# The last block's down product from seven block products instead of eight

## The chip, the cores and the metric

The kernel runs on one core of a Trainium2 chip. A core has TensorE (PE, matrix products into the PSUM memory), VectorE (DVE), ScalarE (ACT), GpSimd (POOL), the queue engine SyncE (SP), and 16 DMA engines that all queues share. The metric is device time in microseconds (us) of one execution; three runs are taken and the median counts.

## What is computed

One layer of a trunk on x of 2048 rows by 1024 columns, in float32: RMSNorm, a combined projection, two attention mixers, gates, an output projection with a residual, and then the part that the change touches:

```python
h2 = _rmsnorm(x, norm2_g[layer])
ff = jax.nn.silu(jnp.einsum('bsd,df->bsf', h2, w_ffn_gate[layer])) * jnp.einsum('bsd,df->bsf', h2, w_ffn_up[layer])
x = x + jnp.einsum('bsf,fd->bsd', ff, w_ffn_down[layer])
return _rmsnorm(x, norm_f_g)
```

The hidden width D_FF is 2816, which is 22 tiles of 128; DEPTH and BATCH are 1.

## The kernel before

The rows are taken in four blocks of 512 (`ROWS`), and the program is written engine by engine, with waits on semaphores; `n(sem, key)` is the count at which the step named by the key is done. A float32 operand is split into a high part and a low part (`hi`, `lo`), and each product is made by three matmuls: high by high, high by low, low by high.

**Weights.** A planned list `JOBS` holds all weight tiles in their order of use, 512 KB each. SP loads job i into one of two buffers `WRAW` as soon as POOL has split job i-2 (L807). POOL (`split`, L984 and L986) waits for the load and for PE's end of job i-2, and then makes, in two halves, `WHI` (a copy, 128x512) and `WLO` (raw minus high, 128x512). PE waits for each half (`w_split`).

**Feed-forward of a block.** The 22 tiles go in three parts of 8, 8 and 6 (`PARTS`). For each tile i of a part, PE makes the gate job ("fg") and the up job ("fu"), 24 matmuls of 128x512 each, into a ring of four PSUM banks ("pair"). ACT takes Silu of the gate bank (L1973), DVE multiplies it with the up bank in place (L2525), ACT copies the product into `FFhi` (L1977), and DVE writes the remainder into `FFlo` (L2528). A gate bank is free again after the Silu, an up bank after `FFlo`.
After the tiles of a part come its down jobs ("fd"): `rows` multiplies the part's `FFhi`, `FFlo` (stationary) with the split weights, two tiles of 512 columns per job, for each half of the 1024 columns and for four row tiles. DVE adds the four finished banks of each half to `X1` (L2470). In a part of 8 these are 8 jobs, in the part of 6 they are 6.

**End.** In the last block ACT squares the rows after the last addition (L1919) and takes the root (L1926), DVE inverts it (L2481); POOL multiplies `X1` with the last norm's weights (L1008) and scales it (L1013) for a half of the columns, DVE does the other half (L2562), and SP stores the rows (L857).

In blocks 0 to 2 DVE and ACT also work on the next block's attention during the feed-forward. In block 3 they do not, and the regions of SBUF that attention uses are free then.

Of the kernel before, what the change touches and what calls it, by code (L numbers as in the profile page):

```python
# [26 lines left out]
P = 128  # L27
# [30 lines left out]
def trunk_program(nc, io, known):  # L58
# [18 lines left out]
    with ExitStack() as ctx:  # L77
# [129 lines left out]
        MGhi, MGlo = at("MGhi", [P, KT, ROWS], f32r, r3), at("MGlo", [P, KT, ROWS], f32r, r3 + 16384)  # L207
        FFhi, FFlo = at("FFhi", [P, SLOTS, ROWS], f32r, r3), at("FFlo", [P, SLOTS, ROWS], f32r, r3 + 16384)
# [5 lines left out]
        def sem(name):  # L214
            return ctx.enter_context(nc.semaphore(name))

        ident_in, const_in, ones_set = sem("ident_in"), sem("const_in"), sem("ones_set")
        ftab_ready, ftab_out, tab_in, taba_ready = (sem(s) for s in ("ftab_ready", "ftab_out", "tab_in", "taba_ready"))
        wu_hi, wu_ready = sem("wu_hi"), sem("wu_ready")
        const_first, eps_set, act_squared, dve_squared, act_scaled = (  # L220
            sem(s) for s in ("const_first", "eps_set", "act_squared", "dve_squared", "act_scaled"))
# [7 lines left out]
        h_ready, h_hi, h_split, h_used = sem("h_ready"), sem("h_hi"), sem("h_split"), sem("h_used")  # L229
        q_hi, q_ready = sem("q_hi"), sem("q_ready")  # L230
        k_hi, k_ready, kw_ready, iw_ready = sem("k_hi"), sem("k_ready"), sem("kw_ready"), sem("iw_ready")
        lat_ready, lat_norm, lat_hi, lat_split = sem("lat_ready"), sem("lat_norm"), sem("lat_hi"), sem("lat_split")
        v_hi, v_ready, vat_ready, carried = sem("v_hi"), sem("v_ready"), sem("vat_ready"), sem("carried")
# [7 lines left out]
        found_ready, tile_signed, big_set, root_loaded = sem("found_ready"), sem("tile_signed"), sem("big_set"), sem("root_loaded")  # L241
# [10 lines left out]
        o_step, o_ready, ot_ready = sem("o_step"), sem("o_ready"), sem("ot_ready")  # L252
# [11 lines left out]
        near_scored, near_masked, near_negmax, near_probs = (sem(s) for s in ("near_scored", "near_masked", "near_negmax", "near_probs"))  # L264
        near_turned, near_hi, near_ready, near_valued = (sem(s) for s in ("near_turned", "near_hi", "near_ready", "near_valued"))
        near_copied, near_summed, near_inverted = sem("near_copied"), sem("near_summed"), sem("near_inverted")
        near_normed, near_kept = sem("near_normed"), sem("near_kept")
        tabb_in, vb_in, comb_ready = sem("tabb_in"), sem("vb_in"), sem("comb_ready")
        out_done = [sem(f"out_done{j}") for j in range(JT)]
# [32 lines left out]

        def ffn_jobs(b, part):
# [4 lines left out]
            return jobs + row_jobs(("fd", part[0]), b, io["w_ffn_down"][0], part)  # L308
# [265 lines left out]
        def _(sp):  # L574
# [219 lines left out]
            for i, (key, src) in enumerate(JOBS):  # L794
# [8 lines left out]
                if width > P:  # L803
                    raw = WRAW[i % 2][:, :, :].rearrange("p (k s) c -> p k (s c)", k=k)
                else:
                    raw = WRAW[i % 2][:, 0:k, 0:width]
# [1200 lines left out]
        def _(dve):  # L2007
# [405 lines left out]
            for b in range(NB):  # L2413
# [101 lines left out]
                for p in range(KT // 2):  # L2515
                    lower_half(1, p)
# [110 lines left out]
```

## Time and profile before

| | |
|---|---|
| median of 3 runs | 3198.29 us (3196.85 to 3199.2) |
| span of the profiled execution | 3196.7 us, 1.6 us under the median |
| granted clock of TensorE | 0.999 of full speed |
| busy share | PE 99%, POOL 64%, DVE 57%, ACT 44% |
| feed-forward of block 3 | from about 2830 us to the end |
| last addition of DVE starts | 3188.35 us |

The span runs from the first to the last instruction; the median of the runs is device time and holds a little more. A busy share is taken over the whole span, so that the stage that is changed has to be read on its own. PE is the only engine that is busy all the time, and matmuls are pipelined: their time is read from the distance of their starts, not from the length of one.

### The profile page before, as it was taken

To read this page: it belongs to the slowest core of one execution; us is meant where nothing else is said; L and a number is where in the kernel's file an instruction comes from. 1 tells how busy PE (TensorE), PEld (TensorE's weight loads), DVE (VectorE), ACT (ScalarE), POOL (GpSimd) and SP (SyncE) were. 2 spreads that over 40 slices of the span, in tenths; PEclk is the share of its full clock that TensorE was granted. 3 is DMA by queue.
4 is the path that set the end of the run, shared out by engine and by line. 5 is a ranking of instruction groups with operands and counts; after the bars stand their busy time and mean duration, and the time that the engine had idled before them with its cause. 6 is when DMAs were issued, how large, how long until landed. Compare 5 with 4: busy or idle time off the path is not lost.

```text
span 3196.7 us, 44024 instructions
## 1 busy us (share of the span) xinstructions
PE 3156.0 (99%) x15678; PEld 2655.0 (83%) x15678; DVE 1814.8 (57%) x3706; ACT 1420.8 (44%) x2589; POOL 2036.0 (64%) x2201
## 2 busy tenths in 40 slices
PE   9999999999999999999999999999999999999998
PEld 7888888878878888888888888988888799888887
DVE  3335546537565545557666666967868689521111
ACT  3324435435473534337354534837655378320001
POOL 5666766665556666764666676366767922666676
PEclk9999999999999999999999999999999999999999
DMA  5765455355615333331533334163333500533332
GB/s 152 198 167 172 119 154 157 103 157 163 209 35 182 102 112 107 108 125 57 201 104 116 103 102 138 28 238 103 98 109 112 171 23 17 180 91 99 95 103 99
DMA packets 464201, 392.59 MB, mean 123 GB/s; under 512 B 29264, under 2 KB 394064, under 8 KB 463344
## 3 DMA queue, kind: packets, MB, share of 16 engines
q1 hardware_dynamic: 442544, 345.56, 36.0%
q10 hardware_dynamic: 21440, 44.22, 3.7%
q8 instruction: 126, 2.06, 0.3%
q14 instruction: 91, 0.75, 0.1%
HBM read 323.76 MB, written 62.81 MB: 121 GB/s over the span
## 4 chain that ended last, share of the span: by engine, by line
PE 92%; POOL 2%; ACT 2%; DVE 2%; issue 1%; DMA 1%; SPq 0%; POOLq 0%; ACTq 0%; DVEq 0%
PE BANK L1049 22%; PE BANK L1051 21%; PE BANK L1050 21%; PE LP L1049 4%; PE LP L1051 4%; PE LP L1050 4%; PE BANK L1330 3%; PE BANK L1355 2%; PE LP L1166 2%; PE LP L1165 2%; PE LP L1310 2%; PE LP L1311 2%; PE BANK L1357 2%; POOL WLO L986 1%; POOL WHI L984 1%
## 5 line engine op out<-in xcount | busy, mean ns | idle before, releaser
L986 POOL TENSOR_TENSOR WLO<-WRAW,WHI 128x512 fp32r<-128x512 f32 x912 | 1213.3, 1330 | 76.0
L984 POOL TENSOR_SCALAR WHI<-WRAW 128x512 fp32r<-128x512 f32 x912 | 639.6, 701 | 776.1 <-PE BANK L1051 622.1
L1049 PE MATMUL BANK<-H2hi,WHI 128*128 128x512 f32 x1376 | 538.7, 392 | 1.1 <-POOL WLO L986 1.1
L1050 PE MATMUL BANK<-H2lo,WHI 128*128 128x512 f32 x1376 | 535.9, 389 | 0.0
L1051 PE MATMUL BANK<-H2hi,WLO 128*128 128x512 f32 x1376 | 535.8, 389 | 0.0
L1049 PE MATMUL BANK<-HThi,WHI 128*128 128x512 f32 (+1 forms) x1024 | 405.1, 396 | 0.8 <-DVE QS L2044 0.5
L1050 PE MATMUL BANK<-HTlo,WHI 128*128 128x512 f32 (+1 forms) x1024 | 399.4, 390 | 0.0
L1051 PE MATMUL BANK<-HThi,WLO 128*128 128x512 f32 (+1 forms) x1024 | 399.3, 390 | 0.0
L1751 ACT ACTIVATE MASK<-SCD,THR 128x896 bf16<-128x896 f32 (+5 forms) x186 | 281.9, 1516 | 191.8 <-DVE THR L2104 164.6
L1051 PEld LDWEIGHTS BANK<-H2hi,WLO 128*128 128x128 f32 x1376 | 258.3, 188 | 54.4
L1049 PEld LDWEIGHTS BANK<-H2hi,WHI 128*128 128x128 f32 x1376 | 258.6, 188 | 53.3 <-issue 1.3
L1050 PEld LDWEIGHTS BANK<-H2lo,WHI 128*128 128x128 f32 x1376 | 258.6, 188 | 51.1
L2071 DVE TENSOR_SCALAR_CACHE_REDUCE MASK<-SCD,THR 128x640 bf16<-128x640 f32 (+2 forms) x192 | 278.1, 1486 | 3.4
L1739 ACT ACTIVATE RB<-LP 128x1024 f32<-128x1024 f32 (+7 forms) x176 | 143.4, 819 | 231.9 <-PE LP L1166 207.9
L2525 DVE TENSOR_TENSOR BANK<-BANK,SL 128x512 f32<-128x512 f32 x88 | 61.2, 696 | 325.7 <-PE BANK L1051 305.9
L2308 DVE SCALAR_TENSOR_TENSOR SCP<-RB,IW,SCP 128x1024 f32<-128x1024 f32 (+7 forms) x140 | 175.2, 1266 | 106.2 <-ACT RB L1739 105.2
L1051 PEld LDWEIGHTS BANK<-HThi,WLO 128*128 128x128 f32 (+1 forms) x1024 | 190.9, 186 | 42.8
L2237 DVE TENSOR_TENSOR PTlo<-BANK,PThi 128x512 fp32r<-128x512 f32 (+1 forms) x296 | 193.2, 659 | 57.5 <-ACT PThi L1680 56.4
L1049 PEld LDWEIGHTS BANK<-HThi,WHI 128*128 128x128 f32 (+1 forms) x1024 | 191.1, 187 | 38.8 <-issue 0.6
L1050 PEld LDWEIGHTS BANK<-HTlo,WHI 128*128 128x128 f32 (+1 forms) x1024 | 191.3, 187 | 36.9
L1633 ACT ACTIVATE LGb<-LGb,NMB 128x1024 f32<-128x1024 f32 (+7 forms) x192 | 174.1, 907 | 57.9 <-POOL NMB L905 54.8
L905 POOL TENSOR_SCALAR NMB<-MXB 128x1 f32<-128x1 f32 x112 | 32.6, 291 | 250.6 <-DVE MXB L2194 247.6
(314 smaller groups left out, 6457.6 us busy)
## 6 DMA issues: line engine op xcount, KB each, us to landing
WRAW<-in_w_in SPq DMA_DIRECT2D x124, 512.0 KB, 4.2
WRAW<-in_w_ffn_gate SPq DMA_DIRECT2D x88, 512.0 KB, 3.8
WRAW<-in_w_ffn_up SPq DMA_DIRECT2D x88, 512.0 KB, 3.8
WRAW<-in_w_ffn_down SPq DMA_DIRECT2D x88, 512.0 KB, 3.5
qsp<-QS SPq DMA_DIRECT2D x32, 512.0 KB, 5.8
WRAW<-in_w_out SPq DMA_DIRECT2D x32, 512.0 KB, 4.6
gates<-GS ACTq DMA_DIRECT2D x62, 256.0 KB, 2.2
GL<-gates ACTq DMA_DIRECT2D x48, 256.0 KB, 4.5
```

The costliest lines, as they stand in the source:

```text
L984: nc.gpsimd.tensor_scalar(hi, raw, 1.0, 1.0, ALU.mult, ALU.mult).then_inc(w_hi, 1)
L986: nc.gpsimd.tensor_tensor(lo, raw, hi.bitcast(f32), ALU.subtract).then_inc(w_split, 1)
L1049: nc.tensor.matmul(dst, whi, mhi, start=first, stop=False)
L1050: nc.tensor.matmul(dst, whi, mlo, start=False, stop=False)
L1051: return nc.tensor.matmul(dst, wlo, mhi, start=False, stop=last)
L1330: last = nc.tensor.transpose(dst[:, 2 * e + h, :], probabilities(b, kind, p, h, t), IDENT[:, :])
L1633: nc.scalar.activation(lg, lg, ACT.Exp, bias=NMB[:, slot, 0:1], accum_out=(ES if s else RS)[:, j, h0:h0 + 1]).then_inc(probs, made(probs, ...
L1739: nc.scalar.activation(RB[:, g % 2, 0:w], logits(("idx",) + key)[:, 0:w], ACT.Relu).then_inc(relu_ready, made(relu_ready, key))
L1751: nc.scalar.activation(mask_of(b)[:, j, 0:w], found_at(b, j)[:, 0:w], ACT.Sign, bias=THR[:, j:j + 1].bitcast(f32), accum_out=CNT[:, j:j + ...
L2071: last = stepped(nc.vector.tensor_scalar(junk[:, j, 0:w], found_at(b, j)[:, 0:w], threshold(j), None, op, ALU.add, accum_out=CNT[:, j:j + 1]))
L2237: nc.vector.tensor_tensor(PTLO[b][r][:, 0:w, :], trans(key)[:, 0:w, :], PTHI[b][r][:, 0:w, :].bitcast(f32), ALU.subtract).then_inc(pt_read ...
L2308: ins = nc.vector.scalar_tensor_tensor(s, r, iw, s, ALU.mult, ALU.add)
```

## The change

In the last block only (`SEVEN`), each part's down product is taken as a product of 2 x 2 blocks and made from seven block products in Strassen and Winograd's way. The left operand's blocks are even and odd tiles of the part by the upper and lower 256 rows; the right operand's are even and odd weight tiles by the two halves of the columns.

- Four of the seven right operands are differences of weight blocks. ACT loads the weights of a part once more, in units of 128x256 from four places, by two DMAs of 256 KB for each unit into one pair of buffers `RQ` (`load_unit`). DVE forms four differences of each unit (`sum_unit`) into `TRAW`; ACT copies them to `THI`, DVE writes the remainders `TLO` over `TRAW` (`lower_t`). There are 8 units in a part of 8 and 6 in the part of 6, two for each pair of tiles. A unit is loaded when the differences of the unit before are done.
- Three of the seven left operands are sums of blocks of the up result. DVE forms them in SBUF (`seven_low`): the product of Silu and up goes to `EVEN` or `ODD` instead of back into its bank, then one 128x256 difference for an even tile and three 128x256 sums for an odd one; ACT copies (`SThi`), DVE takes the remainder (128x768).
- An up bank is free again after that product (`ff_ready`) and no longer after the remainder.
- The other three right operands are plain weight blocks, which SP loads and POOL splits as before: 6 jobs for each part instead of 8 (or 6).
- PE (`seven_products`) makes the first two products in turns, pairs 0 and 1 of both and then the rest of both; each step is 6 matmuls. Two products share two banks and three stay in the bank on top of one another; DVE adds each product to `X1` (`add_products`), and PE waits for the addition two products before.
- At the end the two halves of the columns change places; the last product is made row tile by row tile.
- Some semaphores are merged into others of the same engine.

```diff
+        LEFT = ("a11", 0, 1, 2, "s3", "a12", "a22")
+        RIGHT = ((0, 0), 0, 1, (1, 1), 2, (1, 0), 3)
+        PLACE = (0, 1, 0, 1, 0, 1, 0)
+        OPENS = (True, True, False, False, False, True, False)
+        INTO = ((0, 0), (1, 1), (0, 1), (0, 1), (1, 1), (0, 0), (1, 0))
...
+            if seven(b, part):
+                return jobs + [(seven_key(b, part, m, a), every_other(w, part, *RIGHT[m], a))
+                               for m in range(7) if type(RIGHT[m]) is tuple for a in range(2)]
...
+            def seven_products(b, part):
...
+                steps = [(m, p, range(2)) for ps in (range(2), range(2, count)) for m in range(2) for p in ps]
+                steps += [(m, p, range(2)) for m in range(2, 6) for p in range(count)]
+                steps += ([(6, p, (jj,)) for jj in range(2) for p in range(count)] if part is PARTS[-1]
+                          else [(6, p, range(2)) for p in range(count)])
+                for m, p, jjs in steps:
...
+                    if m > 1 and p == 0 and jjs[0] == 0:
+                        pe.wait_ge(rows_added, n(rows_added, added_key(b, part, m - 2, 1)))
...
+                        pe.wait_ge(t_low, n(t_low, (b, part[0], p, right // 2)))
+                        mhi, mlo = THI[:, p, right, :], TLO[:, p, right, :]
+                    if type(left) is int:
+                        pe.wait_ge(s_low, n(s_low, (b, part[2 * p])))
...
-                        job(H2hi, H2lo, (ff_split, (b, i)), beside=beside_up, ring="pair")
+                        job(H2hi, H2lo, (ff_ready if seven(b, part) else ff_split, (b, i)), beside=beside_up, ring="pair")
...
+                def load_unit(part, u):
...
+                    if u or part[0]:
+                        act.wait_ge(t_summed, n(t_summed, (b, *((part[0], u - 1) if u else (part[0] - SLOTS, SLOTS - 1)), 3)))
...
+                    for h in range(2):
...
+                        act.dma_start(RQ[h][:, :, :], src).then_inc(t_in, 16)
+
+                def seven_high(part, i):
...
+                    if f % 2 == 0:
+                        act.wait_ge(s_made, n(s_made, (b, i)))
+                        nc.scalar.copy(FFhi[:, f, :]...
+                    else:
+                        act.wait_ge(ff_ready, n(ff_ready, (b, i)))
+                        nc.scalar.copy(FFhi[:, f, :], ODD[:, :, :].rearrange("p h r -> p (h r)")).then_inc(ff_hi, made(ff_hi, (b, i)))
+                        act.wait_ge(s_made, n(s_made, (b, i, 2)))
+                        nc.scalar.copy(SThi[:, p, :, :], STR[p // 2][:, p % 2, :, :]).then_inc(s_hi, made(s_hi, (b, part[2 * p])))
+                    if f:
+                        load_unit(part, 2 * f)
+                    p = pair_at(part, f - 1)
+                    if p is not None:
...
+                        for t in range(2):
+                            nc.scalar.copy(THI[:, p, 2 * t:2 * t + 2, :], TRAW[:, p, 2 * t:2 * t + 2, :]
...
+                            if i > part[0]:
+                                load_unit(part, 2 * (i - part[0]) - 1)
+                            seven_high(part, i)
...
+                def sum_unit(part, u):
...
+                    dve.wait_ge(t_in, n(t_in, (b, part[0], u)))
+                    for t, x, y in ((0, RQ[0][:, 1, :], RQ[0][:, 0, :]), (2, RQ[1][:, 1, :], RQ[0][:, 1, :]),
+                                    (1, RQ[1][:, 1, :], TRAW[:, p, 0, c]), (3, RQ[1][:, 0, :], TRAW[:, p, 1, c])):
...
+                        nc.vector.tensor_tensor(TRAW[:, p, t, c], x, y, ALU.subtract
...
+                def seven_low(part, i):
...
+                    if 0 < 2 * f - 1 < len(part):
+                        sum_unit(part, 2 * f - 1)
+                    full(("fu", b, i))
+                    dve.wait_ge(silu_ready, n(silu_ready, (b, i)))
...
+                        nc.vector.tensor_tensor(odd, bk[:, :], gate, ALU.mult).then_inc(ff_ready, made(ff_ready, (b, i)))
+                        dve.wait_ge(ff_ready, n(ff_ready, (b, i)))
+                        for k, x, y, op in ((0, EVEN[:, 2, :], ODD[:, 1, :], ALU.add), (1, raw[:, 0, :], EVEN[:, 0, :], ALU.subtract),
+                                            (2, ODD[:, 0, :], raw[:, 1, :], ALU.subtract)):
...
+                        nc.vector.tensor_tensor(FFlo[:, f, :], odd, FFhi[:, f, :].bitcast(f32), ALU.subtract
...
+                        nc.vector.tensor_tensor(low, raw, SThi[:, p, :, :].bitcast(f32), ALU.subtract
...
+                    if 2 * f < len(part):
+                        sum_unit(part, 2 * f)
+                    if pair_at(part, f + 1 - len(part) // 2) is not None:
+                        lower_t(part, f + 1 - len(part) // 2)
...
+                def add_products(part, before):
...
+                        for jj in range(2):
+                            dve.wait_ge(bank_full, n(bank_full, closed_key(b, part, m, jj)))
...
+                            nc.vector.tensor_tensor(c, bank(("sd", b, part[0], PLACE[m], jj))[:, :], c, ALU.add
```

## Rows read from the trace of the kernel before

**Rows 1.** the page: busy us, share of the span, instructions of each engine

```profile
PE 3156.0 (99%) x15678; PEld 2655.0 (83%) x15678; DVE 1814.8 (57%) x3706; ACT 1420.8 (44%) x2589; POOL 2036.0 (64%) x2201
```

**Rows 2.** stretches of block 3: PE, PEld, DVE, ACT, POOL busy (x), clock, DMA, GB/s

```profile
2900.00:3000.00 100.00, 100.00 (x442) 82.79 (x442) 12.49 (x18) 6.53 (x11) 69.82 (x74) 1.00 0.32 100
...
3100.00:3196.00 96.00, 88.31 (x390) 72.81 (x388) 17.04 (x28) 15.71 (x34) 67.00 (x68) 0.98 0.32 104
```

**Rows 3.** waits of that stage: who waited for whom, us, times, longest

```profile
DVE BANK L2525 <- PE BANK L1051: 188.2, 21, 10.2
...
POOL WHI L984 <- PE BANK L1051: 74.8, 50, 1.5
```

**Rows 4.** timeline, PE: start us, length us, instruction; two matmuls 24 apart

```profile
3180.67 0.39 PE L1049 MATMUL BANK<-WHI,FFhi 128*128 128x512 f32 x1
...
3186.11 0.39 PE L1049 MATMUL BANK<-WHI,FFhi 128*128 128x512 f32 x1
```

**Rows 5.** timeline, POOL: the split of a job (three of four), the next job's start

```profile
3144.96 0.62 POOL L984 TENSOR_SCALAR WHI<-WRAW 128x512 fp32r<-128x512 f32 x1 [1.50 <-PE BANK L1051]
3145.66 1.29 POOL L986 TENSOR_TENSOR WLO<-WRAW,WHI 128x512 fp32r<-128x512 f32 x1
3146.92 0.62 POOL L984 TENSOR_SCALAR WHI<-WRAW 128x512 fp32r<-128x512 f32 x1
...
3150.40 0.62 POOL L984 TENSOR_SCALAR WHI<-WRAW 128x512 fp32r<-128x512 f32 x1 [1.48 <-PE BANK L1051]
```

**Rows 6.** groups by line and shape: busy us, mean ns of one

```profile
L2237 DVE TENSOR_TENSOR PTlo<-BANK,PThi 128x256 fp32r<-128x256 f32 x32 | 13.4, 419 | 3.2 <-ACT PThi L1680 3.2
...
L2525 DVE TENSOR_TENSOR BANK<-BANK,SL 128x512 f32<-128x512 f32 x88 | 61.2, 696 | 325.7 <-PE BANK L1051 305.9 <-ACT SL L1973 19.6
...
L1705 ACT CAST OThi<-OTA 128x512 fp32r<-128x512 f32 x16 | 10.0, 624 | 0.0
...
L1567 ACT ACTIVATE XSQ<-XN 128x1024 bf16<-128x1024 f32 x12 | 12.7, 1055 | 1.0 <-ACT GS L1841 0.4
```

**Rows 7.** ACT's queue: issue of two loads; then loads, KB, us to landing

```profile
2748.95 0.81 ACTq L1699 DMA_DIRECT2D GL<-gates  x2
...
GL<-gates ACTq DMA_DIRECT2D x1, 256.0 KB, 2.9
...
GL<-gates ACTq DMA_DIRECT2D x3, 256.0 KB, 3.4
...
GL<-gates ACTq DMA_DIRECT2D x48, 256.0 KB, 4.5
```

**Rows 8.** timeline, DVE and POOL, where both read operands from SBUF

```profile
66.52 1.29 POOL L986 TENSOR_TENSOR WLO<-WRAW,WHI 128x512 fp32r<-128x512 f32 x1
...
66.92 1.43 DVE L2364 TENSOR_TENSOR AKSlo<-KAT,AKShi 64x512 fp32r<-64x512 f32 x1 [3.56 <-ACT AKShi L1824]
...
69.75 0.62 POOL L984 TENSOR_SCALAR WHI<-WRAW 128x512 fp32r<-128x512 f32 x1 [1.94 <-PE BANK L1051]
...
69.82 1.09 DVE L2364 TENSOR_TENSOR AKSlo<-KAT,AKShi 64x512 fp32r<-64x512 f32 x1
...
70.45 1.61 POOL L986 TENSOR_TENSOR WLO<-WRAW,WHI 128x512 fp32r<-128x512 f32 x1
...
498.27 1.68 DVE L2308 SCALAR_TENSOR_TENSOR SCP<-RB,IW,SCP 128x1024 f32<-128x1024 f32 x1
...
498.96 2.14 POOL L986 TENSOR_TENSOR WLO<-WRAW,WHI 128x512 fp32r<-128x512 f32 x1
...
952.68 1.30 DVE L2225 TENSOR_TENSOR OTlo<-OTB,OThi 128x512 fp32r<-128x512 f32 x2 [3.56 <-ACT OThi L1705]
```

**Rows 9.** timeline of the end, POOL and DVE

```profile
3181.49 6.30 POOL L1008 TENSOR_TENSOR XH<-X,GFB 128x512 f32<-128x512 f32 x5
...
3187.97 4.03 POOL L1013 TENSOR_SCALAR X<-XH,SS 128x1024 f32<-128x1024 f32 x3 [0.18 <-POOL XH L1008]
...
3188.35 0.69 DVE L2470 TENSOR_TENSOR X<-BANK,X 128x512 f32<-128x512 f32 x1 [0.60 <-PE BANK L1051]
```

More of the change, by code:

```diff
@@ L1004, in finish @@
                 pool.wait_ge(gf_in, n(gf_in, b))
-                for half, j in [(0, j) for j in range(JT)] + [(1, 0)]:
+                for half, j in [(1, j) for j in range(JT)] + [(0, 0)]:
                     c = slice(half * ROWS, (half + 1) * ROWS)
@@ L1133, in rows @@
                                 between()
+            def seven_products(b, part):
+                dst = [[take("low", rows_added, added_key(b, part, (6, 5)[place], jj), ("sd", b, part[0], place, jj)) for jj in range(2)]
+                       for place in range(2)]
+                count, jobs = len(part) // 2, {}
+                steps = [(m, p, range(2)) for ps in (range(2), range(2, count)) for m in range(2) for p in ps]
[3 more added lines that the diff above has]
+                for m, p, jjs in steps:
+                    left, right, place = LEFT[m], RIGHT[m], PLACE[m]
+                    if m > 1 and p == 0 and jjs[0] == 0:
+                        pe.wait_ge(rows_added, n(rows_added, added_key(b, part, m - 2, 1)))
+                    if type(right) is tuple:
+                        if p % 2 == 0:
+                            jobs[m, p // 2] = job_no[0]
+                            job_no[0] += 1
+                        i = jobs[m, p // 2]
+                        pe.wait_ge(w_split, 2 * i + p % 2 + 1)
+                        mhi, mlo = (w[i % 2][:, :, :].rearrange("p (k s) c -> p k (s c)", k=2)[:, p % 2, :] for w in (WHI, WLO))
+                    else:
[3 more added lines that the diff above has]
+                        pe.wait_ge(s_low, n(s_low, (b, part[2 * p])))
+                        shi, slo = SThi[:, p, left, :], STlo[p // 2][:, p % 2, left, :]
+                    else:
+                        f = 2 * p + (left in ("a12", "a22"))
+                        pe.wait_ge(ff_split, n(ff_split, (b, part[f])))
+                        c = slice(2 * P, 4 * P) if left in ("s3", "a22") else slice(0, 2 * P)
+                        shi, slo = FFhi[:, f, c], FFlo[:, f, c]
+                    for jj in jjs:
+                        q = slice(jj * P, (jj + 1) * P)
+                        d, end = dst[place][jj][:, :], p == count - 1 and m in (3, 5, 6)
+                        nc.tensor.matmul(d, shi[:, q], mhi, start=(OPENS[m] and p == 0), stop=False, skip_group_check=True)
+                        nc.tensor.matmul(d, shi[:, q], mlo, start=False, stop=False, skip_group_check=True)
+                        last = nc.tensor.matmul(d, slo[:, q], mhi, start=False, stop=end, skip_group_check=True)
+                    if p == count - 1:
+                        last.then_inc(bank_full, made(bank_full, closed_key(b, part, m, jjs[0])))
+                    elif p % 2 and type(right) is tuple:
+                        last.then_inc(bank_full, made(bank_full, seven_key(b, part, m, 0)))
@@ L1919, in square @@
                     nc.scalar.activation(SQJ[:, :], X1[:, j, half * ROWS:(half + 1) * ROWS], ACT.Square,
[L1920 removed]
+                                         accum_out=(SQB if half != (b in SEVEN and stage[0] == "fd") else SQA)[:, j:j + 1]
                                          ).then_inc(rows_squared, made(rows_squared, last_square[0]))
                 def root_row(stage, which, j):
[L1925 removed]
+                    act.wait_ge(rows_squared, n(rows_squared, (b, stage, int(which == 1 or b not in SEVEN), j)))
                     nc.scalar.activation(SS[:, j:j + 1], SQB[:, j:j + 1], ACT.Sqrt, bias=SQC[:, j:j + 1], scale=1.0 / D
@@ L1967, in _ @@
                 for part_no, part in enumerate(PARTS):
+                    if seven(b, part):
+                        load_unit(part, 0)
                     for i in part:
@@ L1994, in _ @@
                             for j in range(JT):
-                                square(("fd", part[0]), half, j)
+                                square(("fd", part[0]), 1 - half if b in SEVEN else half, j)
                                 if half:
@@ L2520, in _ @@
                         near(b + 1, part_no, h)
+                    if seven(b, part):
+                        for i in part:
+                            seven_low(part, i)
+                        add_products(part, before)
+                        before = ("fd", part[0])
+                        continue
                     for i in part:
```

181 lines of the change are left out of this document (137 added, 44 removed).

## The prediction

> **What bounds the kernel now.** I read the views in this order. The page's busy table first: TensorE (PE) is busy 99% of the span, no other engine over 64% [rows 1]. A mean hides stages, so next the stage that is changed, the feed-forward of the last block, in stretches: PE is at 100% until the down products end, and VectorE (DVE) and ScalarE (ACT) are nearly idle there, 12 and 6 us in 100 [rows 2]. The waits of that stage: DVE, ACT and GpSimd (POOL) wait for PE, and PE stands in no line as the one that waits [rows 3]. So in this stage time is worth what PE's work is worth, until something else is late. PE's pace comes from its timeline: two matmuls 24 places apart start 5.44 us apart, 0.227 us each [rows 4]; a job (24 matmuls) is 5.45 us, a gate and an up job, one "tile step" f, 10.90 us. POOL's split of one weight job takes 2 x (0.70 + 1.26) = 3.9 us, then POOL is idle 1.5 us [rows 5].
>
> **What the change removes.** Each part (8, 8 and 6 tiles) makes its down product from 2 x 2 blocks; eight block products become seven. Before: 22 tiles x 8 x 3 = 528 matmuls. After: 7 products x 11 tile pairs x 2 x 3 = 462. 66 x 0.227 = **15.0 us** less, 5.45 per part of 8 and 4.1 for the part of 6, all on the path. POOL's down jobs fall from 22 to 18; off the path, worth nothing as long as POOL's 1.5 us of idle per job lasts.
>
> **What it adds, off PE.** Per part, DVE forms four weight differences for each of 8 (6) units of 128x256, after ACT has loaded the unit in two 256 KB transfers into one buffer; ACT and DVE split them (low halves: two 128x1024 per pair); and DVE forms sums of the up results (three 128x256 per pair, and one for each even tile). PE waits for the up result's product (bank release, two tile steps later) and, at the seventh or eighth step of the products, for the last pair's low sums. Queued behind DVE's wait for a load are that tile's product and all later units; behind ACT's wait for DVE's differences is the next copy of ACT.
> Durations: DVE 0.42 for 128x256 and 0.70 for the product [rows 6]; two independent 512-wide ops in a row end after 1.30 where one takes 0.69 [rows 8], so a follower costs 0.08 less than alone. An added 128x256 is therefore 0.36 in a run, 0.46 where it needs the one before (0.04 for the semaphore); 128x1024 1.14 (1024 at the same rate). ACT 0.62 for 512 and 1.06 for 1024 out of SBUF [rows 6], 768 in between, 0.87.
> The load is not in the trace of before. Nearest: ACT's queue takes 0.81 to issue a pair, the second lands 2.9 after its own issue when nothing else moves, 3.4 beside a load of SP, 4.5 as the median of the whole run [rows 7]. So 3.3 to 4.9 a unit; I take 3.7, between alone and beside SP, whose loads go on every 5.45 us.
>
> **The wait that decides.** Nearly all added DVE operations read two operands from SBUF. Rows 8 show what such an operation and a POOL split do to each other: a DVE subtraction that starts 0.40 after a POOL subtraction takes 1.43 instead of 0.69, so POOL keeps DVE out for 1.12 us of its 1.29; behind POOL's copy it loses 0.40, so that keeps it out for 0.45 of 0.62; and the other way POOL's subtraction takes 1.61 instead of 1.29 behind a 512-wide DVE operation and 2.14 behind a 1024-wide one: DVE keeps POOL out for its element time plus 0.05. Operations with an operand in PSUM, as before the change, cost each other nothing.
> The Trainium skill ("SBUF — State Buffer", section "SBUF: two separate sides") speaks against this change: a DVE operation with two SBUF inputs and a GpSimd operation exclude each other for the whole instruction. The rows bear out that they exclude each other, but for 0.45 of 0.62 and 1.12 of 1.29, not the whole; with whole instructions the mean wait below would be near 0.58 and the sum some 25 us worse.
> The price of one wait: an operation that comes at random meets (0.45² + 1.12²) / 5.45 = 0.27 us on average; one that follows another directly meets a POOL operation that came in between, 0.79 on average, in the 72% of the time in which POOL has work: 0.57. Bounds 0 and 0.57. A run of four differences has one of the first and three of the second kind, 0.50; a run of three 0.47; a pair 0.42. I take **0.45**, and 0.27 for single operations.
> Four differences: 4 x (0.36 + 0.45) = 3.2. Three sums: 3 x 0.91 = 2.7. A pair of low halves: 2 x 1.59 = 3.2. Rest of an even tile after its product: 0.87 + ACT 0.70 + 0.96 = 2.5; of an odd one: 2.7 + 1.0 + 1.4 = 5.15.
>
> **The chain of loads.** Times from the part's first gate job; up job f ends at 10.9 (f + 1). Unit 1 is issued after the Silu of f = 1, at 17.0, lands at 20.7, its differences end at 23.9, product 1 at 24.6 (up job 1 ended at 21.8). Unit 2 waits for the sums and their copy (2.7 + 0.9): issued 28.2, landed 31.9, done 35.1. Unit 3, same buffer: 38.9, done 42.1, product 2 at 42.8 (up job: 32.7). Unit 4: after 1.6 of tile 2, load, differences: done 51.3. Unit 5: 58.2, product 3 at 59.0 (43.6). Unit 6 done 69.5, unit 7 76.5, product 4 at 77.2 (54.5). Each tile step needs two loads and two runs of differences in series, 16 to 18 us where PE takes 10.9; DVE falls behind by 2.8, 10, 15 and 23 us. PE's up job 6 needs product 4's bank at 70.9: **it waits 6.3 us**. Without any waits (0 for 0.45) product 4 would be ready at 61.4, and PE would never notice.
> Then DVE catches up, but not fully: 77.2 + 2.5 + 3.2 (low halves) + 5.85 (tile 5) + 3.2 + 3.2 (tile 6) + 3.2 + 5.85 (tile 7) = 104.2; PE reaches the step that needs it at 87.2 + 6.3 + 7 x 1.36 = 103.0: **1.1 us more**. A part of 8 loses 7.4 and gains 5.45. The part of 6 has no unit 6: product 3 at 59.0 + 5.15 + 3.2 + 3.2 + 3.2 + 5.85 = 79.5, needed at 65.4 + 5 x 1.36 = 72.2: **7.3 lost**, 4.1 gained.
> Other new waits cost nothing: POOL's splits have DVE's holds added, some 32 us per part of 8 (32 x 0.32 + 4 x 0.9 + 4 x 2.4 + 8 x 1.12) against 24 of idle and a lead of 3.5 of the first half of each split, but PE's own 7 us of waiting in the same stretch cover the rest; were DVE never late, POOL would cost 2 to 3 us per part. A product waits for the addition two products before it, 1.4 us of DVE against at least 1.36 of other matmuls; in the last part, where it is that short, PE's 7.3 us stand before it.
>
> **The tail.** Before, POOL ends its last split 6.8 us before PE ends, runs 6.30 us of products with the last norm's weights and 4.03 us of scalings, and ends at 3192.0, 3.7 after PE's last matmul [rows 9]. After, the last weight job can be split only when the fourth product is done and its first job is split, 12.3 - 2.5 us before the end, so that split ends 5.8 before: +1.0 (0 to 1.6).
>
> **Sum.** Stalls 7.4 + 7.4 + 7.3 = 22.1 - 15.0 = +7.1 on PE, +1.0 in the tail: +8.1 us. The profiled execution's 3196.7 becomes 3204.8; the median of the runs stands 1.6 above that span, so 3206.4: **3206 us**. Per 0.03 us of mean wait the sum moves by about 4, per 0.3 us of load by 5.7; with 0.42 it is 3202, with 0.48 or with loads of 4.0 it is 3211 to 3212. Own range 3200 to 3214.
>
> **Rivals.** (A) *The cover holds*: DVE's waits stay at those of random arrival, 0.27. Product 4 is then ready at 70.9, exactly when PE asks, and only about 0.7 us is lost in the last part: -14.3 + 1.0, **3185**. For it: DVE is 88% idle here now [rows 2], the operations need only some 40 of 125 us. Against it: the rows of collisions, and that the new work comes in runs. It decides from a mean wait of 0.30 down. (B) *In between*, wait 0.36: stalls 3.2 + 3.2 + 4.0, -4.7 + 1.0, **3195**, no change that can be seen. (C) *Slow loads*: with 4.5 us, the median of the other stages, seven loads in series add 5.6 to each part of 8: **3222**. Against it: those stages move more than this one. (D) *POOL becomes the bound instead*: DVE on time, splits late by 2.5 per part: -15 + 7.5 + 1, **3192**.
>
> **How the numbers follow.** Forecast 0.46, A 0.20, B 0.16, C 0.12, D 0.06. 0.2% (6.4 us, about what a measurement of this kernel can tell from no change) puts the borders at 3191.9 and 3204.7. Slower: C and nine tenths of the forecast less the part of it below 3204.7 (0.12 + 0.41) = 0.53. Faster: A and half of D, 0.23. Same: the rest, 0.24. The range from 3183.5 to 3214 takes in A, B, D and the forecast's own, and leaves out C and a little more, under 2 in 10; the likeliest case's own range is 3200 to 3214.
>
> **What would show it.** In the profile after: PE matmuls of the last block at 0.227 spacing, 462 of the down products (wrong if the pitch changed); waits of PE on DVE's product of the up result at the seventh tile of the parts of 8, and on DVE's low sums in each part, 7 us a part; DVE's 128x256 differences at a mean near 0.8 us instead of 0.42; ACT's loads landing in about 3.3 to 3.7. If PE shows no waits before 3170 and the differences stay under 0.65, A is right; if PE waits for POOL's split, D.

## The result and the profile after

| | before | after |
|---|---|---|
| median of the runs, us | 3197.6 (5 runs) | 3221.3 (5 runs) |
| profiled execution, span, us | 3196.7 | 3220.7 |
| first matmul of 512 columns (up job of tile 0) to the last matmul, us | 2834.53 to 3187.93 | 2835.29 to 3210.88 |
| from the last matmul's start to the end of the span, us | 8.7 | 9.8 |

The ratio is 1.0065, with an interval of 1.0053 to 1.0077: 0.65% slower. The forecast was 3206 us, with a range from 3183.5 to 3214: slower, as forecast, but 15 us more than forecast, 7 us above the range. It is near the time of rival C, slow loads (3222). The five executions of the changed kernel fall into two groups, 3214.7 to 3215.2 us and 3221.3 to 3222.7, all of them above the range, and the profiled one is the longest; of the six of the kernel with two buffers (below) one took 7538.75 us, from a cause that is not known, and the ratio there leaves it out.

In the waits of the last block's feed-forward PE now stands as the one that waits; before, it stood in no line [rows 3]. Who waited for whom, us in total, times, longest:

```profile
DVE TRAW L2663 <- DMA RQ<-in_w_ffn_down: 59.4, 19, 5.4
...
PE BANK L1102 <- DVE EVEN L2685: 12.0, 2, 6.2
...
PE LP L1222 <- DVE STlo L2711: 7.0, 1, 7.0
...
PE BANK L1102 <- DVE ODD L2699: 4.8, 3, 3.3
...
PE BANK L1102 <- ACT SL L2106: 2.9, 2, 1.7
```

The two waits for EVEN are up job 6 of each part of 8, the wait for STlo is the last pair's low sums in the part of 6: the places that the prediction named. The smaller waits, for ODD (product 3) at up job 5 of each part and for SL (a Silu) at gate job 6 of the parts of 8, it did not have. The first line points to the reason: 19 times DVE itself waited for a load of a unit.

The stage in stretches (PE, PEld, DVE, ACT, POOL busy, clock, DMA share, GB/s):

```profile
2830.00:2960.00 130.00, 120.76 (x535) 98.98 (x535) 76.91 (x94) 25.09 (x38) 86.27 (x84) 0.97 0.40 122
2960.00:3090.00 130.00, 122.33 (x527) 99.81 (x526) 74.88 (x88) 20.47 (x28) 90.28 (x85) 0.97 0.38 114
```

PE was busy in all 100 us of 100 [rows 2] and now lacks 8 to 9 of 130. DVE goes from an eighth to three fifths, and is still far from full: it waits for its loads. The granted clock is 0.97 where it was 1.00.

One link of the chain, in the first part (timeline of DVE, POOL, SP's and ACT's queues; start us, length us, instruction):

```profile
2865.23 2.26 DVE L2663 TENSOR_TENSOR TRAW<-RQ,TRAW 128x256 f32<-128x256 f32 x2
2865.87 1.34 POOL L1039 TENSOR_TENSOR WLO<-WRAW,WHI 128x512 fp32r<-128x512 f32 x1
2867.24 0.37 SPq L860 DMA_DIRECT2D WRAW<-in_w_ffn_up  x1
2867.52 1.21 ACTq L2049 DMA_DIRECT2D RQ<-in_w_ffn_down  x2
...
2872.90 0.42 DVE L2663 TENSOR_TENSOR TRAW<-RQ 128x256 f32<-128x256 f32 x1 [5.41 <-DMA RQ<-in_w_ffn_down]
...
2874.67 0.68 DVE L2685 TENSOR_TENSOR EVEN<-BANK,SL 128x512 f32<-128x512 f32 x1
```

POOL's subtraction holds up the last difference of a unit. When it ends, SP issues the next weight load and DVE ends its run, so ACT issues the next unit's pair of transfers 0.28 us behind SP. DVE's first difference starts 5.38 us later, and behind its four differences stands the product that sets an up bank free. Over the 19 loads that DVE waited for, issue to first difference took 4.52 us on average (3.66 to 5.38). The prediction had 3.7.

The end of the stage on POOL answers to [rows 9]:

```profile
3204.42 1.29 POOL L1039 TENSOR_TENSOR WLO<-WRAW,WHI 128x512 fp32r<-128x512 f32 x1
3205.66 6.72 POOL L1061 TENSOR_TENSOR XH<-X,GFB 128x512 f32<-128x512 f32 x5
3212.56 3.31 POOL L1066 TENSOR_SCALAR X<-XH,SS 128x1024 f32<-128x1024 f32 x3 [0.18 <-POOL XH L1061]
```

The last split now ends 5.6 us before PE (5.8 forecast), and the tail is 1.1 longer (9.8 against 8.7).

**Where the 24 us are.** Between the first matmul of 512 columns and the last matmul lie 375.6 us instead of 353.4: +22.2. In the runs below in which PE waits for nothing, the same stretch takes 338.8 to 339.0, so 36.7 were lost. Of these PE's timeline shows 29.5 in gaps and 6.0 in 30 matmuls that start 0.43 us apart behind the four longest gaps (together 11.6, 10.3 and 13.6 in the three parts); most of the other 1.2 lies in single matmuls around the gaps that start 0.3 to 0.4 us apart. The tail adds 1.1, and 0.8 lies ahead of the stage.

### The profile page after: what moved, and what is told of

Read it like the earlier page. It is cut to its first block, busy times and chain, and to the rows that moved or that the text cites. A ratio compares the mean times of both kernels' runs of the same rounds, so it can differ in the third digit from the quotient of the medians.

```text
span 3220.7 us, 44209 instructions
## 1 busy us (share of the span) xinstructions
PE 3152.3 (98%) x15612; PEld 2648.7 (82%) x15612; DVE 1987.7 (62%) x3889; ACT 1449.7 (45%) x2622; POOL 2043.6 (63%) x2185
## 4 chain that ended last, share of the span: by engine, by line
PE 85%; DVE 5%; DMA 3%; POOL 3%; ACT 2%; issue 1%; ACTq 0%; SPq 0%; POOLq 0%; DVEq 0%
PE BANK L1102 19%; PE BANK L1104 19%; PE BANK L1103 19%; PE BANK L1425 3%; PE LP L1102 3%; PE LP L1104 3%; PE LP L1103 3%; DMA RQ<-in_w_ffn_down 2%; PE BANK L1450 2%; PE LP L1405 2%; PE LP L1406 2%; PE BANK L1452 2%; PE LP L1261 2%; PE LP L1260 2%; DVE TRAW L2663 2%
## 5 line engine op out<-in xcount | busy, mean ns | idle before, releaser
L1777 ACT CAST PThi<-BANK 128x512 fp32r<-128x512 f32 (+1 forms) x296 | 163.9, 560 | 49.7 <-PE BANK L1425 46.9
```

What stands on the lines that cost most here:

```text
L1777: nc.scalar.copy(PTHI[b][r][:, 0:w, :], trans(key)[:, 0:w, :]).then_inc(pt_hi, made(pt_hi, key))
```

## The experiments

The theory after the trace: the sum was right in its mechanism (loads, differences and the product in one chain, with collisions between DVE and POOL), and its load term was too small. The rivals: the collisions alone are the cause; and the slow matmuls behind the long waits cost 6 us that the sum did not have.

Three quantities are compared over the runs. The *load* is the mean time from ACT's issue of a unit to DVE's first difference, over the units for which DVE waited. The *mean wait* is what the 187 two-SBUF operations of DVE took in all beyond their time in the run without splits (107.7 us), divided by 187. *PE lost* is gaps and slow matmuls of the stage (for the filler run, with the 16.3 us of the filler in it).

| kernel | load | mean wait | PE lost | median, us | before, same runs | ratio (interval) |
|---|---|---|---|---|---|---|
| changed kernel | 4.52 | 0.39 | 35.5 | 3221.3 | 3197.6 | 1.0065 (1.0053 to 1.0077) |
| e1 two buffers | not waited for | 0.51 | 0 | 3187.1 | 3198.7 | 0.9962 (0.9949 to 0.9975) |
| e2 no splits | 4.40 | 0 | 0.2 | 3183.4 | 3198.7 | 0.9954 (0.9941 to 0.9967) |
| e3 both | 5.62 (9 units) | 0 | 0.2 | 3183.4 | 3198.7 | 0.9952 (0.9939 to 0.9965) |
| e4 filler | 4.59 | | 35.1 | 3222.7 | 3198.7 | 1.0075 (1.0062 to 1.0088) |
| e5 one load | 3.68 | 0.43 | 21.2 | 3208.1 | 3199.1 | 1.0028 (1.0017 to 1.0038) |
| e6 half the splits | 5.43 | 0.28 | 28.0 | 3216.4 | 3199.1 | 1.0057 (1.0043 to 1.0071) |
| e7 last part alone | 4.72 (4 units) | | 12.7 | 3210.0 | 3199.1 | 1.0034 (1.0022 to 1.0046) |
| e8 no turns | not waited for | | 3.7 | 3189.8 | 3199.1 | 0.9971 (0.9960 to 0.9982) |
| e9 tail | not waited for | | 0 | 3184.0 | 3199.6 | 0.9951 (0.9938 to 0.9965) |

### Two buffers

```diff
-        RQ = [at(f"RQ{h}", ..., (rO, rT + 8192)[h] + 6144) for h in range(2)]
+        RQ = [[at(f"RQ{h}", ..., (rO, rT + 8192)[h] + 6144) for h in range(2)],
+              [at(f"RQB{h}", ..., rX + 24576 + 2048 * h) for h in range(2)]]
...
-                    if u or part[0]:
-                        act.wait_ge(t_summed, ... the unit before ...)
+                    if u > 1:
+                        act.wait_ge(t_summed, n(t_summed, (b, part[0], u - 2, 3)))
...
-                    if f:
-                        load_unit(part, 2 * f)
+                    load_unit(part, 2 * f + 1)
...
-                                load_unit(part, 2 * (i - part[0]) - 1)
+                                load_unit(part, 2 * (i - part[0]))
```

> The whole change, with a second buffer for the operands of the weight sums: odd units land in a stretch of THI that is free until the part's last pair is rounded, and a load is issued one unit further ahead. ScalarE, VectorE and GpSimd do as much as in the changed kernel. Theory (the chain of loads with one buffer makes most of the PE waits): the 4.6 us between a load's issue and the next difference go off the chain, what is left is VectorE's own work beside the port collisions; an event walk with the durations of the changed kernel's trace leaves one PE wait of 2.4 us in the part of 6 and none elsewhere, so no fall of the clock either: some 10 us under the kernel before at the last matmul, with 1.0 more behind it and 0.8 ahead of it about 3189 us (ratio 0.997). Rival (the collisions alone stretch VectorE past PE): the waits of 6 to 7 us stay, 3217 to 3221 us.

Measured: 3187.1 us. PE has no wait in the stage's parts, and its stretches are full again, beside a DVE that is busier than in the changed kernel (PE, PEld, DVE, ACT, POOL busy):

```profile
2830.00:2960.00 130.00, 129.46 (x590) 107.66 (x591) 89.53 (x99) 26.35 (x40) 99.32 (x91) 1.00 0.43 126
2960.00:3090.00 130.00, 130.00 (x575) 107.57 (x575) 86.13 (x90) 21.09 (x29) 98.95 (x91) 1.00 0.41 126
```

The groups of DVE's differences in that run (busy us, mean ns of one):

```profile
L2668 DVE TENSOR_TENSOR TRAW<-RQB,TRAW 128x256 f32<-128x256 f32 x22 | 20.6, 937 | 0.4
L2668 DVE TENSOR_TENSOR TRAW<-RQ,RQ 128x256 f32<-128x256 f32 x11 | 13.3, 1212 | 0.0
```

An operation that takes 0.42 alone takes 0.94 and 1.21 in these two groups and 0.91 on average over all 88 differences: the mean wait rose from 0.39 to 0.51, while POOL is busy for 99 of 130 us instead of 86 to 90. And yet PE loses nothing. So the collisions alone are not the cause; they become one when a load of 4.5 us stands in series with them. The rival of this run falls. Beside the load the second buffer also takes a wait out of ACT's queue, since ACT no longer stands before its next copy until the unit's differences are done; this run does not part the two, and the run with one load of two, below, shows what the load's length alone does. The time is 2 us under the theory's, whose wait of 2.4 us in the part of 6 did not come.

### No splits on GpSimd

```diff
+                if key[0] in ("fg", "fu", "sd") and key[1] == NB - 1:
+                    width = 4
                 for a in range(2):
```

> The changed kernel with one buffer, in which GpSimd rounds and subtracts only 4 of the columns of each weight tile of the last block's feed-forward (the other columns keep what an earlier job left): nearly all of GpSimd's work there is left out, its semaphores and order are kept, and VectorE has no one to share the port with. Theory (loads and collisions add up on one chain): the mean wait per two-SBUF operation goes from 0.45 us to nothing, the chain fits into PE's time, an event walk gives 9 us under the kernel before at the last matmul, about 3190 us. Rival (loads alone: collisions lie beside the loads and cost nothing): the waits of 6 to 7 us stay, 3215 us or more.

Measured: 3183.4 us; PE's only wait in the stage is 0.3 us at its start. DVE waits for its loads even longer than before, and it does not matter. Its groups, and its wait:

```profile
L2665 DVE TENSOR_TENSOR TRAW<-RQ,TRAW 128x256 f32<-128x256 f32 x44 | 18.6, 422 | 0.8
L2672 DVE TENSOR_TENSOR TLO<-TRAW,THI 128x1024 fp32r<-128x1024 f32 x22 | 26.0, 1222 | 0.0
...
DVE TRAW L2665 <- DMA RQ<-in_w_ffn_down: 68.3, 19, 6.5
```

In the changed kernel the same groups were

```profile
L2663 DVE TENSOR_TENSOR TRAW<-RQ,TRAW 128x256 f32<-128x256 f32 x44 | 35.0, 795 | 0.8
L2670 DVE TENSOR_TENSOR TLO<-TRAW,THI 128x1024 fp32r<-128x1024 f32 x22 | 31.6, 1479 | 0.0
```

So the loads alone are not the cause either. Either cause taken away by itself removes all of the 36.7 us: they are two terms of one chain that has to fit into 10.9 us a tile step, and each by itself leaves it short enough. That the run is better than the theory's 3190 shows that the event walk behind that number (a calculation, step by step, of who waits for whom) still had the chain too tight.

### Both

The two edits above together.

> Two buffers, and GpSimd's work of the last block's feed-forward left out as in the run before. Both theories: nothing is left that makes PE wait for VectorE, so this shows what the 66 fewer matmuls give by themselves: 15.0 less in the matmuls, 1.0 more behind the last one and 0.8 ahead, 3184 to 3186 us. If it stays above 3190 there is a cost that neither theory has.

Measured: 3183.4 us, 0.6 under what was expected: from the first matmul of 512 columns to the last matmul it takes 338.8 us (before: 353.4), so the 66 fewer matmuls give 14.6, where 15.0 were forecast. The run with two buffers takes 339.0 there, as long with all collisions as without any. What it has more in its profiled span, 3.3 us, lies for 1.9 behind the last matmul (9.8 against 7.9, where the splits stand ahead of POOL's closing work) and for 1.3 ahead of the stage.

### Filler ahead of the long waits

```diff
+                        if seven(b, part) and i - part[0] == 6:
+                            pe.wait_ge(w_split, 2 * job_no[0] + 1)
+                            fill("low", WHI[job_no[0] % 2][:, 0, :], H2hi[:, 0, :])
                         job(H2hi, H2lo, (ff_ready if seven(b, part) ...
...
+                        if m == 1 and p == count - 1 and part is PARTS[-1]:
+                            fill("pair", FFhi[:, 0, 0:P], THI[:, 0, 0, :])
                         pe.wait_ge(s_low, ...
```

What it is about, in the changed kernel (PE's timeline, around the wait at up job 6 of the first part):

```profile
2903.94 0.39 PE L1104 MATMUL BANK<-H2hi,WLO 128*128 128x512 f32 x1
2910.16 0.80 PE L1102 MATMUL BANK<-H2hi,WHI 128*128 128x512 f32 x1 [5.83 <-DVE EVEN L2685]
2910.75 0.63 PE L1103 MATMUL BANK<-H2lo,WHI 128*128 128x512 f32 x1
2911.18 0.63 PE L1104 MATMUL BANK<-H2hi,WLO 128*128 128x512 f32 x1
...
2914.52 0.40 PE L1103 MATMUL BANK<-H2lo,WHI 128*128 128x512 f32 x1
2914.75 0.39 PE L1104 MATMUL BANK<-H2hi,WLO 128*128 128x512 f32 x1
```

Behind a wait of 5.8 us the matmuls start 0.43 us apart for 4.4 us, near twice the 0.227 of [rows 4]: the granted clock is 0.50 there, the lower level of 1.2 GHz, and then the upper one, 2.4 GHz, again.

> The changed kernel with one buffer, and 24 matmuls (5.4 us) whose results nobody reads put ahead of each of the three long waits of PE (up job 6 of each part of 8, low sums of the last pair in the part of 6). They go into a free bank. Nothing else moves, so the banks come free when they did. Theory (each long idle stretch lowers the granted clock, and about ten matmuls behind it run at 0.43 us): the three waits shrink to 1 to 2 us, the matmuls behind them start 0.227 us apart, 6.1 to 6.7 us less than the changed kernel: 3215 us. Rival (the slow matmuls come of something else, such as their operands): the slow matmuls stay and the time is the changed kernel's 3221 us, or more by what the filler overshoots.

Measured: 3222.7 us. Nothing was gained. The same place, and what follows it a few microseconds later:

```profile
2901.66 5.60 PE L1195 MATMUL LP<-H2hi,WHI 128*128 128x512 f32 x24
2908.24 0.50 PE L1102 MATMUL BANK<-H2hi,WHI 128*128 128x512 f32 x1 [0.98 <-DVE EVEN L2699]
2908.58 0.39 PE L1103 MATMUL BANK<-H2lo,WHI 128*128 128x512 f32 x1
...
2936.80 0.77 PE L1233 MATMUL LP<-THI,SThi 128*128 128x512 f32 x1 [2.39 <-DVE STlo L2725]
```

The filler does what it should: the wait is 1.0 us, and the matmuls behind it start 0.23 apart. But then PE arrives at the last pair's low sums 2.4 us early and waits there; in the changed kernel it had no such wait in the parts of 8. The slow matmuls had lain beside DVE's chain, which sets the time whatever PE does meanwhile. PE lost 35.1 us instead of 35.5, filler included: 0.8 and 0.5 more in the parts of 8 and 1.7 less in the part of 6 (one profiled execution of each kernel). So the expectation of 6 us fell, and so did the rival's first half (behind the fillers of the parts of 8 the slow matmuls did go). In the part of 6 a wait of 3.8 us was left behind the filler, with slow matmuls behind it again, so what they cost there was not measured.

### One load of two

```diff
-                    made(t_in, (b, part[0], u), 32)
+                    h_last = 1 if u or part[0] else 2
+                    made(t_in, (b, part[0], u), 16 * h_last)
...
-                    for h in range(2):
+                    for h in range(h_last):
```

> The changed kernel with one buffer, and of each unit only the first of the two transfers (after the very first unit the lower rows keep what an earlier load left): everything else runs as in the changed kernel. The load term of the prediction's sum is set back near the value that it had there: with the second transfer's issue (0.6 us) and its share of the way gone, 3.4 to 3.7 us from the issue to the first difference where the changed kernel has 4.6. Theory (the sum was right but for the size of that term): the sum's formula, with a mean wait of 0.40 to 0.45 us, gives 5.5 under to 7.2 over the kernel before on PE, and 1.8 more in the tail and ahead of the stage: 3194 to 3207 us, PE's long waits at 0 to 6 us instead of 6.2 to 7.0. Rival (the chain is made by the collisions, a microsecond of load is hidden beside them): 3217 to 3222 us.

Measured: 3208.1 us. The load came out at 3.68 us, the prediction's 3.7, and the time 2 us from the prediction's 3206; it is 1 us above the theory's range of 3194 to 3207. PE's waits:

```profile
PE LP L1222 <- DVE STlo L2712: 7.8, 1, 7.8
PE BANK L1102 <- DVE EVEN L2686: 6.6, 2, 3.4
```

This run decides between the terms. 0.84 us less load took 12 (by the ratios) to 13 us (by the medians) off the time, 4.2 to 4.7 us per 0.3 us, where the prediction had 5.7; the mean wait was a little longer meanwhile, 0.43. The rival, that a microsecond of load is hidden, falls.

### Half of the splits

```diff
+                if key[0] == "fg" and key[1] == NB - 1:
+                    width = 4
                 for a in range(2):
```

> The changed kernel with one buffer, in which GpSimd works on only 4 of the columns of each weight tile of the gate jobs of the last block's feed-forward (the rest is left out); the splits of the up jobs and of the down jobs stay whole. About half of the collisions ahead of the down products go, so that the mean wait falls from 0.40 to about 0.2 us, while the loads stay at 4.6. Theory (the sum's formula: each 0.03 us of mean wait is worth about 4 us, down to a point where the cover holds): 4.7 under the kernel before on PE, 3195 us with what lies around it, between 3187 (0.1) and 3201 (0.25). Rival (every collision costs the same, with no cover): half way between the changed kernel and the one without splits, 3202 us or more.

Measured: 3216.4 us, which neither had. The mean wait fell to 0.28 only, and the loads, which were to stay, took 5.43 us:

```profile
DVE TRAW L2665 <- DMA RQ<-in_w_ffn_down: 79.0, 18, 7.0
PE BANK L1104 <- DVE EVEN L2687: 9.5, 2, 7.3
PE BANK L1104 <- DVE ODD L2701: 6.7, 3, 4.5
PE LP L1224 <- DVE STlo L2713: 4.8, 2, 2.4
```

SP's queue tells why. It loads a weight tile when a split is done; with gate splits that take no time, its loads come in twos:

```profile
2867.26 0.37 SPq L860 DMA_DIRECT2D WRAW<-in_w_ffn_up  x1
2869.52 0.37 SPq L860 DMA_DIRECT2D WRAW<-in_w_ffn_gate  x1
```

where they are 6.1 us apart on average, and 13 of the 18 loads (5.0 to 7.7 us) were issued between two weight loads that start 1.9 to 4.2 us apart. The prediction's rates (5.7 us per 0.3 of load, 4 per 0.03 of mean wait) give with 5.43 and 0.28 17 us over the kernel before on PE and 18 in all; 17 were measured. So the run fails as a test of the mean wait alone, since it changed both terms, but it agrees with a time that follows from the two.

### The last part alone

```diff
-            return b in SEVEN
+            return b in SEVEN and part is PARTS[-1]
```

(and unit 0 of the part no longer waits for a part before it).

> Seven block products in the last part (6 tiles) alone; the two parts of 8 are as before the change. Theory (each part loses its waits by itself, as the trace of the changed kernel shows them for this part: 12.9 us lost, 4.1 gained, 1.0 in the tail): 9.8 over the kernel before, 3208 us. The prediction's step for this part (7.3 lost): 3202 us. Rival (the part of 6 suffers from what the parts before it leave behind): 4.1 - 1.0 under the kernel before, 3195 us.

Measured: 3210.0 us, 10.9 over the kernel before. PE's waits:

```profile
PE LP L1222 <- DVE STlo L2711: 9.3, 1, 9.3
PE BANK L1102 <- DVE ODD L2699: 0.7, 1, 0.7
PE LP L1222 <- DVE FFlo L2691: 0.6, 1, 0.6
```

12.7 us lost by itself, where the changed kernel loses 13.6 in this part; the parts before it leave at most 0.9 behind. The prediction's 7.3 for this part is refuted.

### Without the turns

In the kernel with two buffers:

```diff
-                steps = [(m, p, range(2)) for ps in (range(2), range(2, count)) for m in range(2) for p in ps]
+                steps = [(m, p, range(2)) for m in range(2) for p in range(count)]
```

> Two buffers, with the first two products of each part one after the other instead of in turns. Without turns the third and fourth steps of the first product come two steps (2.7 us) earlier, and with them the second of its weight jobs; the low sums of the last pair are asked for at the same step as before. Theory (the turns give GpSimd's split the time that it needs): PE waits for that split for 1 to 2 us in each part, 2 to 5 us more than with turns, 3189 to 3192 us. Rival (the split is in time either way): 3187 us, no difference.

Measured: 3189.8 us against 3187.1; the intervals of the two ratios overlap, but the trace names the wait, which the kernel with turns does not have:

```profile
PE LP L1224 <- POOL WLO L1041: 2.9, 5, 0.8
```

The turns are worth about 1.2 us in a part of 8 (0.4 and 0.8, for the two halves of the second weight job) and 0.5 in the part of 6; with what starting again costs PE lost 3.7 us. That is the theory's mechanism, at the lower end of its size.

### The last roundings on ScalarE

Two buffers, and:

```diff
-                    nc.gpsimd.tensor_scalar(hi, raw, 1.0, 1.0, ALU.mult, ALU.mult).then_inc(w_hi, 1)
-                    pool.wait_ge(w_hi, 2 * i + a + 1)
+                    if i < len(JOBS) - 2:
+                        ... the two lines above ...
+                    else:
+                        pool.wait_ge(w_late, 2 * (i - len(JOBS) + 2) + a + 1)
...
+                    if part is PARTS[-1] and b + 1 == NB:
+                        for i in range(len(JOBS) - 2, len(JOBS)):
+                            ... waits for the tile's load and for its buffer ...
+                            for a in range(2):
+                                q = slice(a * SLOTS // 2, (a + 1) * SLOTS // 2)
+                                nc.scalar.copy(WHI[i % 2][:, q, :], WRAW[i % 2][:, q, :]).then_inc(w_late, 1)
```

> Two buffers, and the rounding of the last two weight tiles (four copies of 128x512) moved from GpSimd to ScalarE, which is idle there; the subtractions stay on GpSimd. With two buffers the span ends 9.9 us after the last matmul, on GpSimd's chain of last splits, products with the norm's weights and scalings, against 8.1 in the runs without splits. Theory (the last splits set the tail): four copies of 0.65 us leave GpSimd's chain, so it ends up to 1.8 us earlier and the norm's chain on ScalarE and VectorE takes its place: 3185 us, 8.1 to 8.6 us behind the last matmul. Rival (what follows the last matmul on ScalarE and VectorE is as long): 3187 us, no difference.

Measured: 3184.0 us; the span ends 8.5 us behind the last matmul instead of 9.8. This 1.3 is what the change gave; the other half of the profiled spans' difference (3182.8 against 3185.5) lies ahead of the stage, and the intervals of the two ratios overlap. POOL's end with two buffers, and with the roundings moved as well:

```profile
3170.48 6.71 POOL L1063 TENSOR_TENSOR XH<-X,GFB 128x512 f32<-128x512 f32 x5
3177.36 3.31 POOL L1068 TENSOR_SCALAR X<-XH,SS 128x1024 f32<-128x1024 f32 x3 [0.17 <-POOL XH L1063]
```

```profile
3167.00 6.31 POOL L1066 TENSOR_TENSOR XH<-X,GFB 128x512 f32<-128x512 f32 x5
3173.48 2.22 POOL L1071 TENSOR_SCALAR X<-XH,SS 128x1024 f32<-128x1024 f32 x2 [0.18 <-POOL XH L1066]
3177.12 1.25 POOL L1071 TENSOR_SCALAR X<-XH,SS 128x512 f32<-128x512 f32 x1 [1.42 <-DVE SS L2633]
```

POOL's last scaling now waits for the inverse of the root that DVE forms (SS): the norm's chain has taken over, as the theory said. This version is faster than both kernels, by 0.5% than the one before (0.35% to 0.62%) and by 1.1% than the changed one.

## Why the prediction was wrong in its size

**Right: what PE gains.** The matmuls are 66 fewer; with the causes of the waits gone PE's stretch is 14.4 to 14.6 us shorter (e1, e2, e3, e9), where the sum had 15.0.

**Right: the mechanism and its places.** PE waits at up job 6 of each part of 8 for product 4, and in the part of 6 for the last pair's low sums. The chain was forecast to have products 1 to 4 ready at 24.6, 42.8, 59.0 and 77.2 us from the part's start; in the first part they were ready at 27.0, 45.3, 61.0 and 80.1, in the second at 25.3, 43.9, 60.2 and 79.1. DVE falls behind step by step, as worked out there, and stands 0.7 to 2.9 us later. The waits at up job 6 (5.8 and 6.2 us, 6.3 forecast) look better than they are: with the smaller waits ahead of them PE was 9.5 and 8.4 us late by then.

**Right: the mean wait.** 0.45 was taken, 0.39 was measured, far from the 0.27 of rival A. The Trainium skill ("SBUF — State Buffer", section "SBUF: two separate sides") has the two engines shut each other out for the whole instruction, which was worked out to a mean wait near 0.58; the runs agree that they shut each other out (0.39 with GpSimd's splits, none without), and not with its length: in the changed kernel a DVE operation that starts during a subtraction of POOL ends as if it had begun 1.14 to 1.16 us after POOL's start, where the subtraction takes 1.28 to 1.30 (12 cases), and during a copy 0.47 us after it, of 0.62 (2 cases). (By the prediction's own rate the 0.58 would be worth 17 us, not 25.)

**Wrong: the load of a unit, 3.7 us.** This is the term that failed. It was put together from a pair's issue of 0.81, of which half was counted, and a landing between 2.9 and 3.4 [rows 7]. In the stage a pair takes ACT 1.21 us to issue, so the second transfer starts 0.58 behind the first, and the 44 transfers land 2.9, 3.7 and 5.1 us (least, median, most) after their own issue:

```profile
DMA to landing us min/median/max: 2.9/3.7/5.1
```

For the 19 units that DVE waited for, the second transfer lands 3.92 us after its issue on average; with the 0.58 and 0.02 until the difference starts that is 4.52 us. A row of that size stood in [rows 7]: the median of the whole run, 4.5, which was given to rival C with a chance of 0.12 and the argument that other stages move more data. That it fits so well is partly luck, since it is the landing of one transfer behind its own issue, and that is 3.7 in the median here. But the argument overlooked that the loads do not fall at random between SP's weight loads. A weight load starts when POOL has finished a split; the same end of a split lets DVE finish its run of differences, and ACT issues the next unit. Of the changed kernel's 19 loads, the ten slowest (4.42 to 5.38) were issued 0.3 to 1.2 us behind a weight load, and the six fastest (3.66 to 4.07) 2.2 to 4.0 behind one; in the run with one transfer those issued 0.3 behind one took 4.5 to 4.7, all others 2.9 to 3.8. So the collisions seem to put the loads where they are slow. That the two go together is read from the traces; a run that shifts ACT's loads by themselves was not made.

With 4.52 in place of 3.7, and nothing else changed, the prediction's formula gives stalls of 12.0 and 1.1 in each part of 8 and 11.4 in the part of 6: 37.6, where 36.7 were lost, and a time of 3222. One run set the term back to 3.68 and had 3208 (e5), against the prediction's 3206. The agreement is partly luck: with the measured mean wait of 0.39 beside 4.52 the formula gives 30 of the 36.7 us, and 3214. Up to product 4 that is close: it makes PE 9.9 us late at up job 6 (6.3 + 7 x 0.82 for the loads, less 2.1 for the shorter wait), where it was 9.5 and 8.4. What it lacks lies behind, above all in the part of 6 (9.4 against 13.6): there product 3 was ready at 63.2 us and the last low sums at 84.3, forecast at 59.0 and 79.5, and 1.6 us more lie in slow matmuls behind that wait. Why DVE was that late there was not taken apart further.

**Wrong: the range.** The prediction gave 5.7 us for 0.3 us of load and bounds of the load of 3.3 to 4.9, which is over 20 us above the forecast at the upper end; yet the range ended at 3214. It was cut there to leave rival C out. With a sensitivity like that, and a row of 4.5 in hand, the bound belonged in the range.

**Right: the tail and the other covers.** +1.0 was forecast, and 1.1 measured. POOL, rival D, costs one wait of 0.2 us. The prediction said that it would cost 2 to 3 us a part if DVE were never late; with two buffers DVE never was, and PE waited for no split while the turns stood, and without them for 1.2 us a part (e8).

**Not in the sum: the clock.** It falls behind four waits, and 6.0 us of slow matmuls are on PE's account. They were no cost in the parts of 8, where DVE's chain was later anyway (e4); in the part of 6 the run with the filler lost 1.7 us less.

## What to carry to other kernels

Where an added chain on an idle engine nearly fills the time of the busy one, its length is not a cost but a threshold: below it all is hidden, above it each tenth of a microsecond is paid at every step, so look for the link that can be taken off the chain (here a second buffer) before weighing any of them. Take a transfer's time from its neighbours in time, not from its size: what starts it may also start the transfers beside it. And slow matmuls behind a wait cost only where PE is what the next wait is for.

## What the runs showed of the hardware

ACT needs 0.55 us to issue one transfer of 256 KB in rows of 1 KB (e5), 1.21 for two, where the pair in [rows 7] took 0.81.

The granted clock fell to its lower level behind four waits of PE in the changed kernel, of 5.8, 6.2, 7.0 and 3.3 us; behind the last of these the matmuls start 0.43 us apart from 0.7 us after its end on (granted clock 0.50). In other runs it fell behind waits of 2.4 and 3.8 us (e4), 3.3, 3.4 and 7.8 us (e5), 1.8, 4.5 and 7.3 us (e6) and 9.3 us (e7), and did not behind another of 2.4 (e4) and three of 2.1 to 2.5 (e6). The length of the wait alone does not tell.
